# Second layer of a two-block network: another order of the seven products, with band and context scores interleaved by rows

## The reference, cut to what matters

```python
q, k, v, z = jnp.split(u @ w_in, 4, axis=-1)        # u: 768 x 1024, w_in: 1024 x 8192
q = rms_norm(q.reshape(..., NA_HEADS, NA_DH), qn_g)  # each head normalised; k the same
...
s = where(valid, q_r @ k_band + bias, -inf)          # band: 8 rows x 32 columns of keys
s_ctx = q_r @ k_c                                    # 256 context keys
p = softmax(concatenate([s, s_ctx]))                 # one softmax over both
o = p_band @ v_band + p_ctx @ v_c
out = (o * silu(z)) @ w_out
```

## Time and profile before

| | us |
|---|---|
| median of 3 runs | 3306.05 (3302.70 to 3309.83) |
| the profiled execution, its own time | 3304.96 |
| its span, first to last instruction | 3303.1 |
| TensorE busy in the span | 3053.1 (92%) |
| VectorE / ScalarE / GpSimd busy | 1549.1 / 834.9 / 492.6 |

### The profile page before, as it was taken

One profiled execution on the slowest core, in us unless ns is written; L12 is line 12 of the kernel. 1 busy time (PEld: TensorE's weight loads), 2 busy tenths in 40 slices (PEclk: granted clock), 3 DMA queues, 4 the chain that ended last, 5 costly groups with the idle time before them and its releaser, 6 DMA issues. The chain is left out here.

```text
span 3303.1 us, 38110 instructions
## 1 busy us (share of the span) xinstructions
PE 3053.1 (92%) x14382; PEld 1977.1 (60%) x14382; DVE 1549.1 (47%) x3530; ACT 834.9 (25%) x2300; POOL 492.6 (15%) x785
## 2 busy tenths in 40 slices
PE   5999999999999997999999999968999999589699
PEld 2445555555555546777778776547888886244374
DVE  2245455455454336555565554433455564331431
ACT  1013333333333212133232332311212221120131
POOL 1122232132130102212020210000011110110000
PEclk8999999999999998999999999978999999799899
DMA  6420110110121004111212023041211100311001
GB/s 230 170 85 26 34 44 26 43 34 26 51 83 70 1 32 132 59 45 46 58 52 77 26 73 139 1 113 26 52 26 26 52 26 1 108 53 65 26 1 51
DMA packets 138461, 189.21 MB, mean 57 GB/s; under 512 B 22268, under 2 KB 91036, under 8 KB 136228
## 3 DMA queue, kind: packets, MB, share of 16 engines
q1 hardware_dynamic: 137080, 186.70, 17.7%
q10 hardware_dynamic: 1200, 0.09, 0.0%
HBM read 177.10 MB, written 9.67 MB: 57 GB/s over the span
## 5 line engine op out<-in xcount | busy, mean ns | idle before, releaser
L488 PE MATMUL a_psP<-a_w,a_uT 128*128 128x512 f32 x1536 | 700.5, 601 | 7.2 <-DMA a_w<-a_w_in 7.2
L488 PEld LDWEIGHTS a_psP<-a_w,a_uT 128*128 128x128 f32 x1536 | 280.6, 192 | 324.8 <-issue 324.8
L737 DVE TENSOR_REDUCE a_small<-a_psS 128x1 f32<-128x768 f32 (+1 forms) x192 | 140.7, 774 | 402.0 <-PE a_psS L516 402.0
L2236 PE MATMUL d_ps<-d_uT,d_w 128*128 128x264 f32 x1024 | 243.1, 391 | 13.9 <-DVE d_yT L2597 8.6
L2236 PEld LDWEIGHTS d_ps<-d_uT,d_w 128*128 128x128 f32 x1024 | 191.6, 192 | 49.1 <-DVE d_yT L2597 10.6
L1441 PE MATMUL b_psP<-b_w,b_uT 128*128 128x256 f32 x768 | 188.4, 390 | 0.8 <-issue 0.8
L643 ACT ACTIVATE a_e<-a_psS,a_small 128x768 f32<-128x768 f32 (+1 forms) x192 | 143.8, 753 | 139.1 <-DVE a_small L737 138.7
L1441 PEld LDWEIGHTS b_psP<-b_w,b_uT 128*128 128x128 f32 x768 | 145.3, 194 | 26.3 <-issue 7.9
L1759 DVE TENSOR_REDUCE b_small<-b_psS 128x2 f32<-128x512 f32 x64 | 44.2, 690 | 227.0 <-PE b_psS L1494 227.0
L538 PEld LDWEIGHTS a_psO<-a_v,a_pT 128*128 128x128 f32 x896 | 115.1, 192 | 45.9 <-issue 45.9
L650 ACT COPY a_pT<-a_psS 128x768 f32<-128x768 f32 (+1 forms) x96 | 63.0, 656 | 311.4 <-PE a_psS L525 311.4
(11 more groups left out here) (466 smaller groups left out, 5430.2 us busy)
## 6 DMA issues: line engine op xcount, KB each, us to landing
a_w<-a_w_in SPq DMA_DIRECT2D x16, 2048.0 KB, 8.6
b_w<-b_w_in SPq DMA_DIRECT2D x64, 512.0 KB, 4.1
d_w<-a_w_in SPq DMA_DIRECT2D x32, 512.0 KB, 7.2
a_yT<-mod_w SPq DMA_DIRECT2D x8, 1536.0 KB, 8.4
a_yT<-mod_w SPq DMA_DIRECT2D x8, 1024.0 KB, 17.0
b_bias<-bias_table SPq DMA_DIRECT2D x64, 128.0 KB
a_yT<-mod_w SPq DMA_DIRECT2D x8, 512.0 KB, 7.6
a_w<-a_w_out SPq DMA_DIRECT2D x2, 2048.0 KB, 7.8
```

The source lines that it names most:

```text
L488: ins = nc.tensor.matmul(s.psP[:, x % 2, :], s.uT[:, a, t * P:(t + 1) * P], w[:, a, :], start=(a == 0), stop=(a == KD - 1))
L737: nc.vector.tensor_reduce(self.nm[i % 2][:, k:k + 1], self.score_banks(k, keys), AX_X, ALU.max, negate=True).then_inc(self.mx, 1)
L2236: ins = nc.tensor.matmul(ps[:, 4, 0:n], s.w[:, h % 2, b, i, :], s.uT[:, b, half * n:(half + 1) * n], start=(b == 0), stop=(b == KD - 1))
```

## The change

- `ORDER` becomes 1, 2, 6, 5, 3, 7, 4 (products 5 and 3 and 7 change places, 4 is last); the adds follow it. There are eight adds in a step before and after; product 7 has two of them and the last product one.
- The weight sums are called from a new function `add_parts`. T1 of the next block stands behind the add of product 3 and T2 behind that of product 4 of the last step; T3 behind product 2 and T4 behind product 6 of the first step. A sum other than T2 that falls into the early list is held and made at the start of the late list, which is behind `weights`, `evacuate` and `gate`. T2 is made where it falls, after the held ones.
- Quarter b12 is loaded into a place of its own (`s.b12`, in rows of `yT` that are not used until the last group), as soon as T3 of the block before is made. The scratch output of the row squares moves to `s.raw`.
- The squares get a second buffer, and the doubled `z` (`scalar_tensor_tensor`) is made behind `weights`.
- In the score banks, each of 8 rows holds 32 band scores and 32 context scores. One exponential over 512 with one sum takes the place of two over 256 with a sum each, and the `reduce_sum` of the two sums is gone.

```diff
-        self.dump = flat[:, NT * D:(NT + 1) * D]
+        self.dump = s.raw[:, 2:4, :].rearrange("p a n -> p (a n)")
...
+        self.squares = [self.sq[:, :], self.yT[:, 14, :]]
+        self.b12 = self.yT[:, 12:14, :].rearrange("p a n -> p (a n)").rearrange("p (a n) -> p a n", a=4)
...
-    ORDER = (1, 2, 6, 3, 7, 4, 5)
-    READ = (1, 2, 3, 4, 5, 6, 8)
+    ORDER = (1, 2, 6, 5, 3, 7, 4)
+    READ = (1, 2, 3, 4, 5, 7, 8)
...
-    def blocks(self, n):
+    def quarter(self, n):
         a, c = ((0, 0), (4, 0), (4, 1), (0, 1))[n]
-        return slice(a, a + 4), slice(self.H * c, self.H * (c + 1))
+        return a, c, (self.s.b12 if n == 3 else self.s.w[:, a:a + 4, self.H * c:self.H * (c + 1)])
...
         g, k = divmod(b, 4)
-        if b:
+        if b and n < 3:
             before = g * self.N + sum(x[2] for x in self.kinds[:k])
-            sp.wait_ge(self.done, 7 * (before - 1) + (1, 2, 4, 5)[n])
-        rows, cols = self.blocks(n)
-        c0 = (g + self.kinds[k][1] * NG) * GROUP
-        sp.dma_start(self.s.w[:, rows, cols], self.w_in[rows.start * P:rows.stop * P, c0 + cols.start:c0 + cols.stop].rearrange(
-            "(a p) n -> p a n", p=P)).then_inc(self.w_in_sem[n], 16)
+            sp.wait_ge(self.done, 7 * (before - 1) + (1, 2, 5)[n])
+        elif b:
+            sp.wait_ge(self.ts, 4 * (b - 1) + 3)
+        a, c, home = self.quarter(n)
+        c0 = (g + self.kinds[k][1] * NG) * GROUP + self.H * c
+        sp.dma_start(home, self.w_in[a * P:(a + 4) * P, c0:c0 + self.H].rearrange("(a p) n -> p a n", p=P)
+                     ).then_inc(self.w_in_sem[n], 16)
...
+            self.load(sp, b, 3)
             if k == 3 and g:
                 for p in range(3):
                     bias(g, p)
-            for n in range(4):
+            for n in range(3):
...
+            band, ctx = ([self.scores_of(k)[:, :, c:c + 32] for k in range(2)] for c in (0, 32))
             for k in range(2):
-                nc.tensor.matmul(s.psS[:, k, 0:2 * P], s.mask_q[rows[k], :], s.mask_k[rows[k], n, :], start=True, stop=False)
+                nc.tensor.matmul(band[k], s.mask_q[rows[k], :], s.mask_k[rows[k], n, :].rearrange("p (r x) -> p r x", r=ROWS),
+                                 start=True, stop=False)
             for k in range(2):
                 keys = s.kT[rows[k], g % 2, p, first:first + 2 * P].rearrange("p (b r c) -> p r b c", b=4, c=8)
-                nc.tensor.matmul(s.psS[:, k, 0:2 * P], s.qT[rows[k], p, n * P:(n + 1) * P], keys, start=False, stop=True)
+                nc.tensor.matmul(band[k].rearrange("p r (b c) -> p r b c", c=8), s.qT[rows[k], p, n * P:(n + 1) * P], keys,
+                                 start=False, stop=True)
             for k in range(2):
-                nc.tensor.matmul(s.psS[:, k, 2 * P:], s.qT[rows[k], p, n * P:(n + 1) * P],
-                                 s.kT[rows[k], g % 2, p, N_LAT:], start=True, stop=True).then_inc(self.sc, 1)
+                keys = s.kT[rows[k], g % 2, p, N_LAT:].rearrange("p (b r c) -> p r b c", b=4, c=8)
+                nc.tensor.matmul(ctx[k].rearrange("p r (b c) -> p r b c", c=8), s.qT[rows[k], p, n * P:(n + 1) * P], keys,
+                                 start=True, stop=True).then_inc(self.sc, 1)
...
-            self.free(act, f)
+            if f >= 2:
+                self.used(act, f - 2)
             src, fn, scale = (s.z[:, t, :], ACT.Tanh, 0.5) if kind == "z" else (
                 s.raw[:, self.heads_index(g, kind, t) % 4, :], ACT.Square, DH ** -0.5)
-            nc.scalar.activation(s.sq[:, :], src, fn, scale=scale).then_inc(self.sq, 1)
+            nc.scalar.activation(s.squares[f % 2], src, fn, scale=scale).then_inc(self.sq, 1)
...
-                nc.scalar.activation(s.e[:, k, 0:2 * P].rearrange("p (b r c) -> p r b c", b=4, c=8),
-                                     s.psS[:, k, 0:2 * P].rearrange("p (r b c) -> p r b c", b=4, c=8), ACT.Exp,
-                                     bias=self.nm[i % 2][k], accum_out=self.r[i % 2][:, k, 0:1])
-                nc.scalar.activation(s.e[:, k, 2 * P:], s.psS[:, k, 2 * P:], ACT.Exp, bias=self.nm[i % 2][k],
-                                     accum_out=self.r[i % 2][:, k, 1:2]).then_inc(self.ex, 1)
+                nc.scalar.activation(s.e[:, k, :].rearrange("p (b r c) -> p r b c", b=8, c=8),
+                                     s.psS[:, k, :].rearrange("p (r b c) -> p r b c", b=8, c=8), ACT.Exp,
+                                     bias=self.nm[i % 2][k], accum_out=self.r[i % 2][:, k:k + 1]).then_inc(self.ex, 1)
...
+        b11, b21, b22, b12 = (self.quarter(i)[2] for i in range(4))
         t1, t2, t4 = (s.wt[:, i, :, :] for i in range(3))
+        t3 = s.w[:, 0:4, self.H:]
...
-            ins = nc.vector.tensor_tensor(b12, b22, b12, ALU.subtract)
+            ins = nc.vector.tensor_tensor(t3, b22, b12, ALU.subtract)
...
-        if kind in "kq" and p in (2, 7):
-            before = self.heads_index(g, kind, 2 * pr + (p == 7)) - 4
+        if kind in "kq" and p in (2, 5):
+            before = self.heads_index(g, kind, 2 * pr + (p == 5)) - 4
             if before >= 0:
                 dve.wait_ge(self.tp, before + 1)
-        if p == 5 and self.chunk(x)[2] and self.chunk(x)[0] + 1 < 4 * NG:
-            for i in (1, 2):
-                self.weight_sum(dve, self.chunk(x)[0] + 1, i)
...
+        elif p == 5:
+            dve.wait_ge(self.parts, n + 3)
+            nc.vector.tensor_tensor(c22, part, ps, ALU.add).then_inc(self.parts, 1)
         elif p == 3:
-            dve.wait_ge(self.parts, n + 3)
-            nc.vector.tensor_tensor(c12, part, ps, ALU.add).then_inc(self.parts, 1)
+            dve.wait_ge(self.parts, n + 4)
+            nc.vector.tensor_tensor(c12, c22, ps, ALU.add).then_inc(self.parts, 1)
         elif p == 7:
-            nc.vector.tensor_tensor(c22, part, ps, ALU.add).then_inc(self.parts, 1)
-        elif p == 4:
-            dve.wait_ge(self.parts, n + 5)
-            nc.vector.tensor_tensor(c21, c22, ps, ALU.subtract).then_inc(self.parts, 1)
+            nc.vector.tensor_tensor(c22, c22, ps, ALU.add).then_inc(self.parts, 1)
+            nc.vector.tensor_tensor(c21, part, ps, ALU.add).then_inc(self.parts, 1)
         else:
-            nc.vector.tensor_tensor(c22, c22, ps, ALU.add).then_inc(self.parts, 1)
-            nc.vector.tensor_tensor(c12, c12, ps, ALU.add).then_inc(self.parts, 1)
-        if p in (1, 2) and self.chunk(x)[1]:
-            self.weight_sum(dve, self.chunk(x)[0], 2 + p)
+            dve.wait_ge(self.parts, n + 7)
+            nc.vector.tensor_tensor(c21, c21, ps, ALU.subtract).then_inc(self.parts, 1)
+    def add_parts(self, dve, i, early):
+        if not early:
+            for b, n in self.held:
+                self.weight_sum(dve, b, n)
+            self.held = []
+        for j in (self.early if early else self.late)[i]:
+            self.add_part(dve, j)
+            p = self.ORDER[j % 7]
+            b, first, last = self.chunk(j // 7)
+            n = 0
+            if last and b + 1 < 4 * NG and p in (3, 4):
+                b, n = b + 1, {3: 1, 4: 2}[p]
+            elif first and p in (2, 6):
+                n = {2: 3, 6: 4}[p]
+            if n == 2 or (n and not early):
+                for held in self.held:
+                    self.weight_sum(dve, *held)
+                self.held = []
+                self.weight_sum(dve, b, n)
+            elif n:
+                self.held.append((b, n))
...
-            nc.vector.tensor_reduce(self.m_ctx, s.psS[:, 0:2, 2 * P:], AX_X, ALU.max).then_inc(self.cm, 1)
+            ctx = s.psS[:, 0:2, :].rearrange("p k (r x) -> p k r x", r=ROWS)[:, :, :, 32:]
+            nc.vector.tensor_reduce(self.m_ctx, ctx, mybir.AxisListType.XY, ALU.max).then_inc(self.cm, 1)
...
-                rows = "p (r x) -> p r x"
-                sc = s.psS[:, k, 0:2 * P].rearrange(rows, r=ROWS)
+                sc = self.scores_of(k)[:, :, 0:32]
...
             dve.wait_ge(self.ex, 2 * i + 2)
-            nc.vector.reduce_sum(self.sums, self.r[i % 2], AX_X).then_inc(self.su, 1)
-            dve.wait_ge(self.su, i + 1)
-            nc.vector.reciprocal(self.rr, self.sums).then_inc(self.rc, 1)
+            nc.vector.reciprocal(self.rr, self.r[i % 2]).then_inc(self.rc, 1)
...
-        def use_squares(g, kind, t, f):
-            dve.wait_ge(self.sq, f + 1)
+        def sum_squares(g, kind, t, f):
             if kind == "z":
-                z = s.z[:, t, :]
-                nc.vector.scalar_tensor_tensor(z, s.sq[:, :], 1.0, z, ALU.add, ALU.mult).then_inc(self.zdone, 1)
                 return
             j = self.heads_index(g, kind, t)
-            nc.vector.reduce_sum(self.ss[:, j % 2, :], s.sq[:, :].rearrange(view, h=HG), AX_X).then_inc(self.red, 1)
+            dve.wait_ge(self.sq, f + 1)
+            nc.vector.reduce_sum(self.ss[:, j % 2, :], s.squares[f % 2].rearrange(view, h=HG), AX_X).then_inc(self.red, 1)
...
             if kind == "z":
+                dve.wait_ge(self.sq, f + 1)
```

(44 more changed lines are left out.)

## The result

The changed kernel takes 3315.3 us (median of 8 runs, 3308.9 to 3322.0) against 3305.8 us before: ratio 1.0026, 95% interval 1.0015 to 1.0037. It is slower by some 9 us (ratio of the medians 1.0029). The profiled execution took 3313.19 us (3304.96 before), with a span of 3311.4 us. One of the four runs of e8, further down, took 4732 us at a granted clock of 0.62, and its ratio leaves that run out.

What follows compares the result with a forecast made beforehand. TensorE, busy 92% of the span, was taken as the bound, so only its waits and low clock could change; 3304.96 us less 42.4 removed plus 45.0 added gave 3307.6, so 3308 us, range 3284 to 3322.

Steps and rivals of the forecast that it cites:

- no visible change: Outcome that the time stays between 3299.4 and 3312.7 us, not to be told from before; chance 0.39.
- Softmax waits, 33.1 us: TensorE's 18 waits for scaled softmax weights, in turns that finish two tiles, all go: gain 33.1 us.
- Clock behind them, 8.4 us: Work lost to TensorE's lowered clock after softmax waits of 3.1 to 3.4 us comes back: gain 8.4 us.
- Product order, 3.1 us for T2 and 0.8 for T3: New product order shortens TensorE's waits for weight sums T2, gain 3.1 us, and T3 of block 0, gain 0.8 us.
- Six stalls for T4, 34.9 us: TensorE waits for held T4: 5.0 us in turn -15, 5.8 in -9 and -5, 6.1 in 8, 24 and 40.
- Clock behind each stall, 2.1 us, 12.6 in all: Lowered TensorE clock after each of the six T4 stalls costs 2.1 us more; bounds 1.7 and 3.3.
- Turns 10 to 12, 3.0 us left: Held T1, T3 and T4 come late in turns 10 to 12: 1.0 us a group kept as loss, 3.0 us.
- T2 in turns -10 and -6, 0.9 us: T2 of the q and v blocks stands behind three adds there: 0.45 us each, 0.9 us added.
- the one costed at nothing: In turns 8, 24 and 40 the gate between scaling and T4 counted 0.2 us; no wait for the gate was priced.
- The rival with shorter stalls: The six T4 stalls cost under 37 us and the change wins: 3262.6 with none, middle case 3288; chance 0.22.
- The rival of more waits: Held sums delay maxima and weights in turns 9 to 12, so TensorE stalls more: 3323 us; chance 0.13.
- Rows that cost: Writing or reading scores in rows takes longer and softmax waits return in part: 3325 us; chance 0.05.

Runs made afterwards that it cites:

- e8: Kernel before with only the new product order, held sums and b12's home, but T4 made at once and never held: 3288.5 us, 0.9941.
- e5: Kernel before with only the second squares buffer and the doubled z behind the softmax weights: 3278.5 us, 0.9920.
- e6: Kernel before with only band and context scores in rows, one exponential over both and no sum of two sums: 3290.0 us, 0.9955.
- e7: Kernel before with only the new product order, the held weight sums and the home for b12: 3315.4 us, 1.0028.
- e3: Changed kernel with the gate ahead of the scaling of heads in turns that finish k or q tiles, T4 still held: 3298.8 us, 0.9975.
- e1: Changed kernel with T4 made where it falls, behind the add of product 6, and never held: 3273.4 us, 0.9910.
- e4: Changed kernel with both edits, T4 made at once and the gate ahead of the scaling of heads: 3256.3 us, 0.9856.

## Why the prediction was right in kind, and where its sum was off

The direction and place of the two large effects were right, and 3315.3 us lies in the range, but the sum was low: 3307.6 against 3313.2 in the profiled execution, +2.6 against +8.2. By the threshold that I had set, the median counts as slower, to which I had given 0.36; no visible change had 0.39. In the layer itself the miss is larger. From its first matmul to the scores of turn 63 it is 10.5 us longer than before (11.27 - 0.75), 7.9 more than the sum. The rest of the program took some of that back: 0.8 us more ahead of the layer, 0.7 less in turn 63, and 2.3 less behind, in code that the change does not touch. That part of the agreement is luck.

- *Softmax waits, 33.1 us: go.* Right, all 18. The exponential over 512 takes 0.68 us and its sum's read 0.20; 0.73 and 0.2 were assumed. What removes them is less simple than I wrote: each of the three parts removes some of them alone (e5 24.9 us, e6 10.7, e7 18.5), and they overlap.
- *Clock behind them, 8.4 us.* Right in size. In the table the difference falls by 4.57 us from turn 11 to turn 12. Of this 3.34 - 1.54 = 1.80 is waiting, since a wait for the gate now stands there, so 2.8 us is clock. The other five long waits (turns 2, 18, 27, 34, 43) give 0.2, 0.2, 1.2, 1.8 and 1.2 us in the same way, 7.5 in all. Behind turns 2 and 18 the granted clock was 1.00 over the 10 us that follow, so their 0.2 us are not clock but what starting again after a wait takes; behind the short waits, too, 0.14 to 0.24 us came back each time, another 2.1.
- *Product order, 3.1 us for T2 and 0.8 for T3.* Measured 3.0 and 0.8.
- *Six stalls for T4, 34.9 us.* Measured 34.9 us. That the totals agree so well is luck: the terms were 5.0, 5.8 twice and 6.1 three times, and 5.0, 4.9 twice and 6.7 three times were measured, so that an error of -1.8 and one of +1.8 cancel. In turns -9 and -5 T4 came ahead of the gain and took 1.2 us; in turns 8, 24 and 40 it came second and took 2.3. In turn -15 it met no gain. The Trainium skill's rule on this (page "SBUF — State Buffer", section "Who interferes with whom") is borne out in both orders: 2.30 us for T4 where the gain began first, and 1.21 us, with 2.19 for the gain, where T4 did.
- *Clock behind each stall, 2.1 us, 12.6 in all.* In the turns below 0 the 8 records behind the stall took 3.75, 3.75 and 3.41 us instead of 1.89. In turns -15 and -9 the low clock outlasted them, and up to where the records have their old length again it is 2.6, 2.4 and 1.5 us. With the 3.9, 1.6 and 1.9 of turns 8, 24 and 40 this makes 13.9 us, 1.3 more than the sum has.
- *Turns 10 to 12, 3.0 us left.* The one wait there is 0.15 us, in turn 11, for T2. Too dear by 2.9.
- *T2 in turns -10 and -6, 0.9 us.* Measured 1.7 (0.84 and 0.85).
- **The step that failed is the one costed at nothing: what stands behind the scaling of heads besides T4.** I named `gate(i-1)` as work between the scaling and T4 and never asked who waits for it. TensorE's value products do. Before, the softmax weights were so late that the scalings ran without waiting for GpSimd, and the gate was in time. With early weights VectorE waits for GpSimd inside the turn, the second scaling meets the first gain, and the gate is 0.5 to 1.5 us late in turns 4, 6, 10 and 11 of three groups: 10.7 us. e5 shows that they come with the squares, e3 that they are on the path. This one term, less the 2.9 us above, is 7.8 of the 7.9 us. The smaller misses (T2 +0.8, clock behind the stalls +1.3, what came back behind the old waits about -1, last group -1.0) cancel.
- In the last group each turn is 0.08 us shorter than before, 1 us in sum, not forecast. The eight transposes of the softmax weights take 1.04 instead of 1.09 us there and begin 0.03 us earlier; why is not shown.
- *The rival with shorter stalls* did not come about in this kernel; e1 is what it would have looked like. *The rival of more waits* was right that there were more, but they stood in another place. *Rows that cost* fell with e6.

## What to carry to other kernels

Work put off until "after the urgent part" of a turn is put off until after everything that stands there, waits for other engines included. So ask which wait ends last ahead of the new place (here a chain of 6.7 us through GpSimd), and who needs the result in the same turn. An engine with 40% idle time (VectorE here) can still be late with every result, because it works in order; when one thing on its queue gets earlier, look at each thing behind the next wait, and ask who waits for that. Parts that shorten one and the same wait do not add up; parts that remove different waits do (e4).

## What the runs showed of the hardware that was not expected

T4, one VectorE instruction over 128x1024 with two inputs in SBUF, took 1.21 or 2.30 us depending on 0.2 us in the start of a GpSimd instruction of 1.26 us; the one that came second lost the time. In all three pairs looked at, the second did all but 0.15 us of its own time after the end of the first: T4 (1.22 us alone) ended 1.09 us after the gain in turn 8, the gain (1.26 alone) 1.13 us after T4 in turn 8 of e3, and the scaling (0.69 alone) 0.55 us after the gain in turn 4.

A stall of 6.72 us cost 3.9, 1.6 or 1.9 us more through the clock, with the granted clock at 0.57, 0.83 and 0.79 in the 10 us from its end (turns 8, 24 and 40), for one and the same program. Six waits of 3.07 to 3.35 us in the kernel before cost 0.2 to 2.8 us more behind them: 0.2 in the two after which the granted clock stayed at 1.00, and 1.2 to 2.8 where it was 0.83 or 0.66.
